# Ten units instead of fifteen beside the gated recurrence, five in pieces beside the matrix memory

## What is computed

```
proj = rmsnorm(x) @ w_in + b_in                      # 28 blocks of 128 columns, and 8 gate columns
h_m  = mlstm(m_q, m_k, m_v, m_i, m_f)                # matrix memory, 4 heads of 64
y_m  = head_rmsnorm(h_m) * sigmoid(m_o)
y_c  = c_b * causal_dwconv(c_c * c_h, sconv_w)       # short convolution
y_a  = moba_attention(a_q, a_k, a_v, rel_bias)       # block attention, 4 heads
f    = lb + (1 - lb) * sigmoid(h_f)
o_h  = hgrn2(silu(h_q), 1 - f, log(f), h_i)          # gated recurrence, 4 heads
y_h  = head_rmsnorm(o_h) * silu(h_g)
y    = concat(y_m, y_c, y_a, y_h) @ w_out
```

## Time and profile before

| | |
|---|---|
| median of three runs | 2371.46 us |
| the profiled execution | 2366.57 us |
| its span, first to last instruction | 2364.8 us |
| mean granted TensorE clock | 0.975 |
| TensorE matmul busy | 2212.6 us, 94% |
| VectorE busy | 1047.7 us, 44% |
| ScalarE busy | 849.3 us, 36% |
| GpSimd busy | 814.0 us, 34% |

### The profile page before, as it was taken

One profiled execution on the slowest core, in us unless ns is written; L12 is line 12 of the kernel. 1 busy time (PEld: TensorE's weight loads), 2 busy tenths in 40 slices (PEclk: granted clock), 3 DMA queues, 4 the chain that ended last, 5 costly groups with the idle time before them and its releaser, 6 DMA issues.

```text
span 2364.8 us, 27132 instructions
## 1 busy us (share of the span) xinstructions
PE 2212.6 (94%) x10016; PEld 1730.0 (73%) x10016; DVE 1047.7 (44%) x1558; ACT 849.3 (36%) x1266; POOL 814.0 (34%) x343
## 2 busy tenths in 40 slices
PE   6788989879999998898899999999999998999999
PEld 5676367657888885575678888878778876788887
DVE  3455564557552525437533222235562565322121
ACT  5333343443222223345543323343432443433231
POOL 3322023314444443220244444443234323444443
PEclk9899999989999999998999999999999999999999
DMA  3212013112332333110123222332222211223233
GB/s 140 67 54 72 33 40 104 66 36 84 116 111 98 98 129 98 43 60 18 42 93 98 94 95 97 98 105 72 71 72 89 72 63 63 90 97 98 98 98 98
DMA packets 54967, 193.36 MB, mean 82 GB/s; under 512 B 6096, under 2 KB 6352, under 8 KB 54480
## 3 DMA queue, kind: packets, MB, share of 16 engines
q1 hardware_dynamic: 50400, 181.58, 23.4%
q10 hardware_dynamic: 4464, 10.36, 1.4%
HBM read 189.82 MB, written 2.10 MB: 81 GB/s over the span
## 4 chain that ended last, share of the span: by engine, by line
PE 72%; issue 14%; DVE 9%; POOL 4%; ACT 1%; DMA 0%; POOLq 0%; DVEq 0%; SPq 0%; ACTq 0%
PE gemm_ps L489 21%; PE gemm_ps L491 21%; PE gemm_ps L490 21%; POOL wl L458 4%; PE out_ps L816 2%; DVE tmp L1519 1%; DVE arena L1867 1%; PE turn_ps L644 1%; DVE tmp L1874 1%; PE out_ps L654 1%; PE score_ps L635 1%; DVE x L1541 1%; DVE xl L1519 1%; PE score_ps L808 1%; DVE arena L1519 1%
## 5 line engine op out<-in xcount | busy, mean ns | idle before, releaser
L458 POOL TENSOR_TENSOR wl<-raw,wh 128x1024 fp32r<-128x1024 f32 x339 | 813.8, 2402 | 1532.8 <-ACT wh L1042 1532.7
L489 PE MATMUL gemm_ps<-xh,wh 128*128 128x512 f32 x1512 | 614.5, 406 | 56.5 <-DVE xl L1519 23.4
L1042 ACT ACTIVATE wh<-raw 128x1024 fp32r<-128x1024 f32 x339 | 358.8, 1059 | 781.3 <-DMA raw<-w_in 756.1
L490 PE MATMUL gemm_ps<-xl,wh 128*128 128x512 f32 x1512 | 594.4, 393 | 0.0
L491 PE MATMUL gemm_ps<-xh,wl 128*128 128x512 f32 x1512 | 594.3, 393 | 0.0
L490 PE MATMUL gemm_ps<-arena_r,wh 128*128 128x512 f32 (+1 forms) x1124 | 432.3, 385 | 0.0
L489 PEld LDWEIGHTS gemm_ps<-xh,wh 128*128 128x128 f32 x1512 | 287.8, 190 | 140.4 <-issue 57.4
L489 PE MATMUL gemm_ps<-arena_r,wh 128*128 128x512 f32 (+1 forms) x868 | 334.4, 385 | 11.0 <-DVE arena_r L1524 10.0
L490 PEld LDWEIGHTS gemm_ps<-xl,wh 128*128 128x128 f32 x1512 | 287.4, 190 | 66.3 <-issue 8.8
L491 PE MATMUL gemm_ps<-arena_r,wl 128*128 128x512 f32 (+1 forms) x868 | 332.6, 383 | 0.0
L491 PEld LDWEIGHTS gemm_ps<-xh,wl 128*128 128x128 f32 x1512 | 287.1, 190 | 61.2
(11 more groups left out here) (294 smaller groups left out, 2044.9 us busy)
## 6 DMA issues: line engine op xcount, KB each, us to landing
raw<-w_in SPq DMA_DIRECT2D x339, 512.0 KB, 3.3
arena<-na_in ACTq DMA_DIRECT2D x14, 256.0 KB, 2.7
x<-x_in SPq DMA_DIRECT2D x8, 256.0 KB, 6.1
out<-x ACTq DMA_DIRECT2D x8, 256.0 KB, 2.7
arena<-alibi_in ACTq DMA_DIRECT2D x6, 256.0 KB, 3.5
con<-con_in SPq DMA_DIRECT2D x1, 1432.0 KB, 11.2
arena<-moba_in ACTq DMA_DIRECT2D x1, 1024.0 KB, 4.8
arena<-mem_in ACTq DMA_DIRECT2D x1, 1024.0 KB, 4.7
```

Source lines behind the costliest of these rows:

```text
L458: pool.tensor_tensor(wl[:, k, :], raw[:, k, :], wh[:, k, :].bitcast(F32), ALU.subtract).then_inc(unit_split, 1)
L489: pe.matmul(o, wh[:, n % RING, w], h[:, kt, 0:width], start=(kt == 0), stop=False)
L490: pe.matmul(o, wh[:, n % RING, w], l[:, kt, 0:width], start=False, stop=False)
L1042: act.activation(wh[:, k % RING, :], raw[:, k % RING, :], ACT.Copy).then_inc(high_split, 1)
```

## The change

- Three units ahead of the first pair of heads as before, and two ahead of the second; units at levels 1, 3, 5 of the first pair and 2, 4 of the second, ten in all.
- The other five are fed to TensorE k-tile by k-tile (`feed`, three matmuls each): one whole unit at the start of `mlstm`, then two k-tiles at four places in each of the four heads. VectorE evacuates one unit per head, ScalarE adds its bias behind the head's exponentials.
- The gate rows are made in three parts: `forget_sums` ahead of the fifth evacuation, `gate_rows_made` ahead of the sixth, `gate_limits` behind it. The memsets of the score weights go behind the eighth evacuation.
- ScalarE raises units 4 and 5 ahead of the gates' bias and of the gates' logarithm.
- The transposes of the gate rows and their copy move from `mlstm` into `hgrn`; the transposes of the attention's values move to the last head of `mlstm` and behind it; the sigmoid of the output gates moves from head 1 to head 3.
- The second short convolution goes from item 7 of the attention to item 10.

The diff, with context cut:

```diff
@@ -88,14 +88,18 @@
-FILL_START, FILL_LEVELS = 3, (0, 1, 2, 3, 4, 5)
+FILL_AHEAD, FILL_LEVELS = (3, 2), ((1, 3, 5), (2, 4))
+FILL_HGRN = sum(FILL_AHEAD) + sum(map(len, FILL_LEVELS))
+FILL_MLSTM = 5
 W_IN_P = 28
...
 BESIDE = {0: 15, 2: 16, 3: 17, 4: 18, 5: 19}
-assert FILL_START + 2 * len(FILL_LEVELS) + len(BESIDE) == len(LATER_BLOCKS)
+assert FILL_HGRN + FILL_MLSTM + len(BESIDE) == len(LATER_BLOCKS)
@@ -683,14 +687,37 @@
+            fed = [FILL_HGRN * KT]
+            def feed(count):
+                for _ in range(count):
+                    n, kt = later_unit(fed[0] // KT), fed[0] % KT
+                    if kt == 0:
+                        pe.wait_ge(unit_split, n + 1)
+                        pe.wait_ge(emptied, n - 1)
+                    o, w = gemm_ps[:, n % 2, :], slice(kt * P, (kt + 1) * P)
+                    pe.matmul(o, wh[:, n % RING, w], xh[:, kt, :], start=(kt == 0), stop=False)
+                    pe.matmul(o, wh[:, n % RING, w], xl[:, kt, :], start=False, stop=False)
+                    m = pe.matmul(o, wl[:, n % RING, w], xh[:, kt, :], start=False, stop=(kt == KT - 1))
+                    if kt == KT - 1:
+                        m.then_inc(unit_done, 1)
+                    fed[0] += 1
+            def turn_attended(b):
+                for t in range(T):
+                    m = pe.transpose(turn_ps[:, 0, t * P:(t + 1) * P], proj1[:, A_V + b, t * P:(t + 1) * P], ident)
+                m.then_inc(turned_v, 1)
             def mlstm():
-                take(gate_rows)
-                for t in range(T):
-                    m = pe.transpose(score_ps[:, 0, 4 * t:4 * t + 4], gate_b[0:4, t * P:(t + 1) * P], ident[0:4, 0:4])
-                m.then_inc(cols_turned, 1)
-                pe.wait_ge(bias_added, len(FIRST_BLOCKS) + 12)
-                turn_values([proj1[:, b, :] for b in (M_V, M_V + 1, A_V, A_V + 1)])
-                take(cols_ready)
+                pe.wait_ge(bias_added, len(FIRST_BLOCKS) + 6)
+                for b in range(2):
+                    for t in range(T):
+                        m = pe.transpose(turn_ps[:, b, t * P:(t + 1) * P], proj1[:, M_V + b, t * P:(t + 1) * P], ident)
+                    m.then_inc(turned_v, 1)
+                feed(KT)
+                take(copied_v, 2)
                 take(gate_rows)
@@ -706,6 +733,11 @@
                     for j in range(T + 2):
+                        if 1 <= j <= 4:
+                            feed(2)
+                        if j == 1 and h == 3:
+                            pe.wait_ge(bias_added, len(FIRST_BLOCKS) + 12)
+                            turn_attended(0)
                         if j < T:
@@ -720,6 +752,8 @@
                 take(scores_used, 2)
+                take(copied_v)
+                turn_attended(1)
@@ -763,9 +798,13 @@
                 turn_values([proj1[:, H_I, :], proj1[:, H_I + 1, :]])
-                fill(FILL_START - 1)
+                take(gate_rows)
+                for t in range(T):
+                    m = pe.transpose(score_ps[:, 0, 4 * t:4 * t + 4], gate_b[0:4, t * P:(t + 1) * P], ident[0:4, 0:4])
+                m.then_inc(cols_turned, 1)
                 for b in range(2):
+                    fill(FILL_AHEAD[b] - (b == 0))
                     take(level_ready)
@@ -784,6 +823,8 @@
                             take(scores_used, 2)
+                        elif b == 0:
+                            take(cols_ready)
                         for j in range(T):
@@ -791,7 +832,7 @@
                                     m.then_inc(scores_ready, 1)
-                        if lev in FILL_LEVELS:
+                        if lev in FILL_LEVELS[b]:
                             fill()
@@ -1203,12 +1244,17 @@
                 step(act.activation(gate_a[f, :], gate_a[f, :], ACT.Exp, scale=-1.0))
+                raise_to(5)
                 act.activation(gate_b[f, :], gate_a[f, :], ACT.Ln, bias=1.0).then_inc(gate_logs, 1)
+            def copy_attended(b):
+                take(turned_v)
+                act.activation(values_moba[:, :, b * P:(b + 1) * P],
+                               turn_ps[:, 0, :].rearrange("p (t c) -> p t c", c=P), ACT.Identity).then_inc(copied_v, 1)
             def mlstm():
-                take(cols_turned)
-                act.activation(small[:, 32:48], score_ps[:, 0, 0:16], ACT.Identity).then_inc(cols_ready, 1)
-                copy_values([v[:, :, b * P:(b + 1) * P] for v in (values1, values_moba) for b in range(2)])
+                copy_values([values1[:, :, b * P:(b + 1) * P] for b in range(2)])
                 take(gate_sums)
@@ -1216,7 +1262,9 @@
                     m.then_inc(gate_fun, 1)
-                    if h == 1:
+                    fill()
+                    if h == 3:
+                        copy_attended(0)
                         act.wait_ge(bias_added, len(FIRST_BLOCKS) + 14)
@@ -1226,6 +1274,8 @@
                 m.then_inc(recurrence_copied, 1)
+                copy_attended(1)
+                fill()
                 act.dma_start(arena[:, 28 * N:32 * N], mem_in).then_inc(memory_in, 16)
@@ -1264,6 +1314,8 @@
                 copy_values([values1[:, :, b * P:(b + 1) * P] for b in range(2)])
+                take(cols_turned)
+                act.activation(small[:, 32:48], score_ps[:, 0, 0:16], ACT.Identity).then_inc(cols_ready, 1)
                 take(gate_arg)
@@ -1273,8 +1325,7 @@
                     act.activation(small[:, 24:28], g[:, P - 1:N:P], ACT.Exp).then_inc(gate_fun, 1)
-                    if not b:
-                        fill(FILL_START)
+                    fill(FILL_AHEAD[b])
                     take(gate_arg)
@@ -1290,10 +1341,10 @@
                             act.activation(edge[:, 2, :], edge[:, 3, :], ACT.Exp).then_inc(gate_fun, 1)
-                            raise_to(later_unit(FILL_START + len(FILL_LEVELS) * b + lev - 1) + 3)
-                        if lev - 2 in FILL_LEVELS:
+                            raise_to(later_unit(filled[0]) + 3)
+                        if lev - 2 in FILL_LEVELS[b]:
                             fill()
-                    fill(sum(lev in FILL_LEVELS for lev in (5, 6)))
+                    fill(sum(lev in FILL_LEVELS[b] for lev in (5, 6)))
                 take(weights_used)
@@ -1379,6 +1430,7 @@
             act.wait_ge(emptied, FIRST["in"] + 1)
+            raise_to(4)
             step(act.activation(gates[0:HD, :], gates[0:HD, :], ACT.Identity, bias=p_("b_gates", 0, 0, HD)))
@@ -1690,20 +1742,25 @@
-            def gate_rows_made():
-                f, r = slice(32, 36), slice(0, 4)
-                one = edge[:, 0, :]
+            def forget_sums():
+                f = slice(32, 36)
                 take(gate_logs)
...
-                done(dve.tensor_tensor_scan(gate_a[f, :], one[f, :], gate_g[f, :], 0.0,
+                done(dve.tensor_tensor_scan(gate_a[f, :], edge[f, 0, :], gate_g[f, :], 0.0,
                                             ALU.mult, ALU.add))
+            def gate_rows_made():
+                f, r = slice(32, 36), slice(0, 4)
                 done(dve.tensor_copy(gate_g[r, :], gate_a[f, :]))
                 done(dve.tensor_tensor(gate_b[r, :], gates[r, :], gate_g[r, :], ALU.subtract), gate_rows)
-                done(dve.tensor_tensor_scan(gate_a[r, :], one[r, :], gate_b[r, :], 0.0,
+                done(dve.tensor_tensor_scan(gate_a[r, :], edge[r, 0, :], gate_b[r, :], 0.0,
                                             ALU.mult, ALU.max))
+            def gate_limits():
+                r = slice(0, 4)
                 done(dve.tensor_tensor(gates[r, :], gate_g[r, :], gate_a[r, :], ALU.add), gate_sums)
@@ -1770,9 +1829,11 @@
                     scaled(n, o)
+                forget_sums()
+                scaled(*first[4])
                 gate_rows_made()
-                for w in weights:
-                    done(dve.memset(w, 0.0))
+                scaled(*first[5])
+                gate_limits()
                 reset = edge[:, 3, :]
@@ -1780,8 +1841,10 @@
                     done(dve.tensor_tensor_scan(g, reset, g, 0.0, ALU.mult, ALU.add), gate_arg if b else dve_step)
-                for n, o in first[4:]:
+                for n, o in first[6:]:
                     scaled(n, o)
+                for w in weights:
+                    done(dve.memset(w, 0.0))
                 take(gate_fun)
@@ -1824,9 +1886,9 @@
                                  level_ready if a is q else dve_step)
-                        if lev - 1 in FILL_LEVELS:
+                        if lev - 1 in FILL_LEVELS[b]:
                             fill()
-                    if 6 in FILL_LEVELS:
+                    if 6 in FILL_LEVELS[b]:
                         fill()
@@ -1971,6 +2033,7 @@
                         mixer_out(b)
+                if i == 10:
                     dve.wait_ge(bias_added, len(FIRST_BLOCKS) + 20)
```

## The result

The changed kernel takes 2403.51 us, median of four runs (2397.76 to 2404.96), the kernel before 2370.71 beside it (2369.45 to 2375.95). The ratio is 1.0134, 95% interval 1.0118 to 1.0150: slower, by 32.8 us where 22.7 were forecast, and 1.5 us beyond the upper end of the range (2402). The profiled execution took 2404.96 us (span 2403.1, granted clock 0.962) against 2366.57 (span 2364.8, 0.975).

A forecast was written before the change was run, and what follows sets the result against it. The prediction took TensorE to bound the kernel. Its terms -10.7, -1.5, +13.0, -4.5, +3.0, +24.6 and -1.2 sum to +22.7, which added to 2371.5 gives 2394 us; range 2372 to 2402.

The forecast's parts named there:

- Rival (a): The clock holds through the 3.6 us waits at the levels: +0.4 us, 2372; at some places only, up to 2378; chance 0.12.
- Rival (b): Unit pieces in the matrix memory are almost free, its stage shrinking by 7.0 us: total -8.9, 2363; chance 0.08.
- Rival (c): The start is not freed, some 5 us of wait stay: that part is -5, total +28.4, 2400; chance 0.08.
- Rival (d): Matrix memory's clock oscillates too, three more heads running slow like the first, 3 x 3.1 us: 2403; chance 0.04.
- Start, -10.7: Up to the third unit ahead: TensorE's 8.57 us wait and low clock behind it go, 10.7 us less.
- Levels of the first pair, -1.5: Recurrence levels with units only at 1, 3, 5: waits of 3.6 us, mostly low clock behind them, 1.5 us less.
- Two units ahead of the second pair, +13.0: In front of the second pair's far blocks: two units cost 11.2 us, the stretch to level 0 another 2.0.
- Levels of the second pair, -4.5, tail +3.0: Levels with units only at 2 and 4: 4.5 us less; levels 6, 7 and products at lower clock: 3.0 more.
- Matrix memory, +24.6: Five units enter: 27.3 us of matmuls and 1.3 of restarts, less 3.6 of idle time filled and smaller savings.
- The restarts: In the matrix memory, restarting one whole unit and 16 six-matmul pieces: 1.3 us, bounds nothing to 2.5.
- The first head: Matrix memory's first head, 3.1 us slow before, given an even chance to stay fast; part of a -0.1 term.
- Attention, -1.2: Moving the convolution shrinks TensorE's wait for item 7 to 4.6 us, splits ending where they did: 1.2 us less.

The follow-up runs named there:

- experiment 5: Also `warm_levels`: changed kernel plus dummy matmuls that nothing reads at the recurrence levels without a unit; 2391.26 us, ratio 1.0077.
- experiment 1: Also `start_only`: kernel before with only the change's start (gate rows in three parts, memsets later, units 4 and 5 raised early); 2359.26 us, ratio 0.9956.
- raise_before_item0: Changed kernel with one of ScalarE's raises made at the end of the matrix memory instead of in the attention's item 0; 2404.39 us, ratio 1.0145.
- two_ahead: Also experiment 6: kernel before with two units moved from levels 0 and 1 of the second pair to ahead of that pair; 2385.31 us, ratio 1.0060.
- start_warm: Kernel of experiment 1 plus dummy matmuls in waits ahead of the first pair, at the far blocks and before the matrix memory's first head; 2352.61 us, ratio 0.9920.
- late_conv_only: Also experiment 2: kernel before with only the second short convolution moved from item 7 of the attention to item 10; 2374.11 us, ratio 1.0017.
- whole_units: Also experiment 3: changed kernel with each matrix memory head getting its unit whole instead of in four pieces; 2397.18 us, ratio 1.0117.
- experiment 7: Kernel of experiment 5 plus nine dummy matmuls in the 2.21 us wait ahead of the matrix memory's first head; 2383.74 us, ratio 1.0053.
- experiment 8: Kernel of experiment 7 with the second convolution put back from item 10 to item 7 of the attention; 2379.96 us, ratio 1.0043.
- start_warm_tail: Kernel of start_warm plus five dummy matmuls behind each group of levels 6 and 7 of both pairs; 2348.00 us, ratio 0.9904.

## Why the prediction was right and wrong

The direction stood, and of the mechanism this: five units moved to places where TensorE has no room, and waits opened at the levels, with the low clock behind them. What failed is the price of the pieces and of the first head in the matrix memory, and the attention, where the collisions with GpSimd were not priced. Rival (a), a clock that holds, would have needed 1.00 at the levels; the rows have 0.80 and 0.70, and experiment 5 prices that and the tails at 13 us. Rival (b), pieces that are nearly free, needed a stage near 50 us; it is 77. Rival (c) fell with experiment 1. Rival (d) named nearly the measured time, but not the place: heads two to four have clock 1.00 and 15.6 us each.

The steps of the sum, one by one:

- **Start, -10.7**: -11.55 here, -10.64 alone. Right, within what profiles differ by.
- **Levels of the first pair, -1.5, and the tail behind them, not in the sum**: -3.36 and +2.37, together -1.0. The levels gave more because a group with its unit behind a wait took 8.35 to 8.55 us, where I took 9.0. The tail was left out because a unit stands at level 5; its waits of 1.64 let the clock fall all the same, in this profile and in those of `start_only`, `raise_before_item0`, `two_ahead` and `start_warm` (+2.34 to +2.36 each time), not in those of `late_conv_only` and of `whole_units`, where the levels took 2.7 more instead. These two places trade with each other; one profile doesn't settle either.
- **Two units ahead of the second pair, +13.0**: +12.42, and +12.28 alone (experiment 6). Right.
- **Levels of the second pair, -4.5, tail +3.0**: -3.62 and +3.08. Right within 1 us.
- **Matrix memory, +24.6: mis-sized, +28.83.** Two terms of the sum were too small. *The restarts*, "I take 1.3" from bounds of 0 to 2.5: the second and third head grew by 15.61 - 10.24 = 5.37 each. 24 matmuls are 5.45, and a wait of 1.12 was filled, so four pieces pay (5.37 + 1.12 - 5.45) / 4 = 0.26 each to start; experiment 3 gives 0.3. For sixteen pieces this is 4.2, beyond the upper bound, which had been taken from the restart of a whole unit. *The first head*, "an even chance to stay fast", part of a term of -0.1: the 2.21 us wait that had slowed it before was seen to stay, and it alone decides (experiment 7). The head takes 20.22 now, 4.61 over the next one, since 24 more matmuls stand in the slow stretch; before it took 12.37, which is 3.25 over the work of the next one (10.24 less its wait of 1.12). So the low clock there costs 1.4 more than before. An outcome with a known cause had been given as a chance. The filled idle time, 3.6, was right (1.12 in the second and in the third head, 0.24 in the fourth, the other 1.1 ahead of the first). 27.3 of matmuls, 4.3 of restarts and 1.4 of clock less 3.6 make 29.4; the small transposes and copies gave back the last 0.6, where 0.3 was forecast.
- **Attention, -1.2: the wrong sign, +6.38.** The step that failed is one that the sum does not have: ScalarE's and GpSimd's raises were priced nowhere in the attention, though the earlier trace rows had shown a 2.36 on four partitions and rival (c) had even named GpSimd for it. Two operations of VectorE are held beside GpSimd's. The first costs 3.65 up to the scores of the next item: waits of 1.12 and 1.00 for one of 0.22, and 1.7 for the clock behind them (3.68 against 1.98). The second, among the last splits, goes with the convolution's move and makes the other 2.7 (2.90 in experiment 2, 4.0 with some clock in experiment 8). The step had said that the splits end where they did, because the convolution "only changes place with them"; on VectorE that is so, up to the 2.20 that one cast was held (experiment 2). Behind this cast TensorE's last three steps took 4.01 us at the low clock, where they had taken 2.04. Without these 4.2 us the stage of experiment 2 would have shrunk by 1.3, as forecast. That is an estimate: no run moves the convolution and keeps GpSimd off the splits, and the clock might have fallen behind the wait of 1.68 alone. But each of the six profiles with the convolution at item 10 has one split of 2.56 to 2.86 us, and none of the six with it at item 7 has one over 0.8.
- **The rest**: the profiled execution lost another 3.8 us after 382, in small steps, with no instruction changed there. `whole_units`, alike there, took 1.8 less than the kernel before. That points to a difference between executions; what made it stays open.

The Trainium skill's page "SBUF — State Buffer", section "Who interferes with whom", says that VectorE and GpSimd share one pair of ports as an exclusive lock, and that of two operations that want it the one issued first keeps it to its end and the other is blocked. The traces agree with the blocking: 2.58 instead of 0.61, 2.72 and 2.63 instead of 0.69 and 0.43, each begun within 0.25 us behind a GpSimd operation of 2.35 to 2.41 us and ended 0.3 to 0.6 us behind its end. No run here shows which port it is.

## What to carry to other kernels

Before taking work out from under a chain of waits, price the clock behind the new waits and not only the waits: here the clock behind seven waits of 3.1 to 3.7 us, tails included, cost 13 us that dummy work gave back. A moved operation is priced not only by what becomes the last one ahead of TensorE, but by what it makes earlier on the other engines: here the move was neutral on VectorE and brought GpSimd's operation onto a split. And where a slow stretch has a known wait ahead of it that stays, it stays slow, the longer the more work is put into it; filling that wait with matmuls nobody reads is the cheaper edit.

## What the runs showed that I had not expected

- A wait of 1.64 us ahead of the products let the clock fall in some profiles (3.76 to 4.54 us for sixteen products instead of 2.37) and not in others of the same code ahead of it; the wait of 2.21 us ahead of the first head did in every profile that has it.
- Dummy matmuls at half clock are no longer shorter than the wait they stand in: twelve took 4.75 us instead of 3.02 and delayed level 1 by 1.5 us.
- A piece of six matmuls among those of the matrix memory pays 0.26 us to start, more than the 0.15 of a whole unit in the recurrence.
- A VectorE operation on two columns takes 2.33 us when it starts beside GpSimd's (0.17 alone).
- `start_warm_tail` was put together from experiments 1, 5 and 7: 22.7 us faster than the kernel before by the ratio, with 55 matmuls that nothing reads and the start of the change without the rest of it.
